# Where a small projection's weights are swept: from TensorE in the scan to VectorE in the feed-forward stages

## What is computed

```python
def ada_params(cond, w, b):                       # cond (1, 1024), w (1024, 6144), b (6144)
    m = jax.nn.silu(cond) @ w + b
    return jnp.split(m[..., None, :], N_MOD, axis=-1)

for i in range(DEPTH_2):                          # 2 layers
    sh_m, sc_m, gt_m, sh_f, sc_f, gt_f = ada_params(c, ada_w[i], ada_b[i])
    if kind == 0 or ctx_live:                     # layer 0 alone
        csh_m, csc_m, cgt_m, csh_f, csc_f, cgt_f = ada_params(c_ctx, ada_w[i], ada_b[i])
    h = modulate(x, norm_mix[i], sh_m, sc_m)      # rmsnorm(x, g) * (1 + scale) + shift
```

## Time and profile before

| | |
|---|---|
| runs | 2309.95, 2308.20, 2309.11 us; median 2309.11 |
| span of the profiled execution, first to last instruction | 2304.8 us |
| TensorE, VectorE, ScalarE, GpSimd busy | 91%, 27%, 20%, 11% of the span |
| bytes moved | 575.5 MB, 250 GB/s over the span |

### The profile page before, as it was taken

One profiled execution on the slowest core, in us unless ns is written; L12 is line 12 of the kernel. 1 busy time (PEld: TensorE's weight loads), 2 busy tenths in 40 slices (PEclk: granted clock), 3 DMA queues, 4 the chain that ended last, 5 costly groups with the idle time before them and its releaser, 6 DMA issues. The chain is left out here.

```text
span 2304.8 us, 25911 instructions
## 1 busy us (share of the span) xinstructions
PE 2107.9 (91%) x10718; PEld 1359.1 (59%) x10718; DVE 623.4 (27%) x1420; ACT 461.7 (20%) x899; POOL 252.8 (11%) x385
## 2 busy tenths in 40 slices
PE   8999899999999998878889998888889899998897
PEld 6854587678878755667674443333478644333334
DVE  4566340232213235743231110011111311111101
ACT  2222231222213345444320000000111200000001
POOL 2034120111112133000100000000000001000000
PEclk9999999999999999989889999999899899999998
DMA  7479644334432221110269999999924699999994
GB/s 251 146 325 412 249 146 146 109 128 146 146 99 73 74 73 37 37 38 2 110 248 380 428 428 427 427 427 428 380 100 154 280 379 427 428 428 427 428 428 188
DMA packets 105042, 575.51 MB, mean 250 GB/s; under 512 B 5536, under 2 KB 28665, under 8 KB 75225
## 3 DMA queue, kind: packets, MB, share of 16 engines
q1 hardware_dynamic: 103455, 570.59, 61.6%
q10 hardware_dynamic: 970, 2.23, 0.3%
q0 software_dynamic: 496, 0.97, 0.2%
HBM read 572.72 MB, written 1.05 MB: 249 GB/s over the span
## 5 line engine op out<-in xcount | busy, mean ns | idle before, releaser
L3094 PE MATMUL ex_u<-ring,ex_xt 128*64 128x512 f32 x1024 | 235.1, 614 | 29.2 <-DMA ring<-in_w 27.8
L3094 PE MATMUL ex_u<-ring_extra,ex_xt 128*64 128x512 f32 x1024 | 233.5, 610 | 28.5 <-DMA ring_extra<-in_w 28.5
L784 PE MATMUL linear_ps<-hT,ring 128*128 128x256 f32 x960 | 211.8, 383 | 8.5 <-PEq L444 6.4
L784 PEld LDWEIGHTS linear_ps<-hT,ring 128*128 128x128 f32 x960 | 184.4, 193 | 35.5 <-issue 8.5
L3094 PEld LDWEIGHTS ex_u<-ring,ex_xt 128*64 128x64 f32 x1024 | 82.6, 141 | 178.2 <-issue 178.1
L3094 PEld LDWEIGHTS ex_u<-ring_extra,ex_xt 128*64 128x64 f32 x1024 | 80.5, 141 | 178.7 <-issue 178.1
L2151 PE MATMUL dl_front<-dn_src,ring 128*128 128x256 f32 (+1 forms) x512 | 176.5, 501 | 2.4 <-DVE dp_cv L2318 2.4
L3200 DVE TENSOR_TENSOR ex_hid<-ex_sil,ex_u 128x512 f32<-128x512 f32 x32 | 34.8, 1086 | 490.0 <-PE ex_u L3094 490.0
L1570 PE MATMUL ffn_ps<-hT,ring 128*128 128x256 f32 x704 | 153.9, 382 | 4.3 <-PEq L677 4.3
L1570 PEld LDWEIGHTS ffn_ps<-hT,ring 128*128 128x128 f32 x704 | 134.9, 192 | 23.3 <-issue 4.7
L2151 PEld LDWEIGHTS dl_front<-dn_src,ring 128*128 128x128 f32 x512 | 99.4, 199 | 65.1 <-issue 57.6
(11 more groups left out here) (617 smaller groups left out, 2679.5 us busy)
## 6 DMA issues: line engine op xcount, KB each, us to landing
ring_extra<-in_w SPq DMA_DIRECT2D x88, 2048.0 KB, 25.4
ring<-in_w SPq DMA_DIRECT2D x88, 2048.0 KB, 25.5
ring<-in_ada_w SPq DMA_DIRECT2D x16, 2048.0 KB, 15.9
ring<-in_ffn_w_up SPq DMA_DIRECT2D x22, 1024.0 KB, 6.5
ring<-in_w_in SPq DMA_DIRECT2D x8, 2048.0 KB, 9.2
ring<-in_ada_w SPq DMA_DIRECT2D x16, 1024.0 KB, 14.7
ring<-in_w_in_a SPq DMA_DIRECT2D x8, 2048.0 KB, 8.5
ring<-in_w SPq DMA_DIRECT2D x16, 1024.0 KB, 7.2
```

The costliest lines, as they stand in the source:

```text
L784: mm = pe.matmul(ps[:, q % banks, 0:n], w[:, k, j * P:(j + 1) * P], src[:, k, 0:n], start=k == 0, stop=k == kc - 1)
L3094: mm = pe.matmul(u[H * a:H * a + H, i, :], xt[:, b, k, H * a:H * a + H], cols, start=k == 0, stop=k == KC - 1, skip_group_check=True)
```

## The change

Layer 0's 12 ada tiles stay in the scan. Layer 1's 12 are taken out of the scan and the stick-breaking stage, with the second row copy and turn. They are queued between the feed-forward weights, and VectorE sweeps them: in 48 steps of 128x1024 it multiplies each weight row by its partition's value of silu(c) and adds it to one array of 128x6144 (K.cond, Sweep.step). 22 steps stand in the up stage, one behind each chunk's convolution; 26 in the down stage, 4 ahead of the context's move, 10 behind it, and 12 behind context.scale. Then TensorE sums over the partitions (12 products with a column of ones, Sweep.sum, ahead of the last six f), ScalarE copies the row, TensorE turns it after c = 1, and VectorE finishes mods and gains of layer 1 after c = 3. A slot that held a swept tile is free when its four steps are done (K.swept_at).

With U0 to U10 for the tiles of w_up, D0 to D5 for those of w_down and S0 to S11 for the swept ones, the queue is now U0 S0 U1 U2 S1 U3 U4 S2 U5 U6 S3 U7 U8 S4 U9 U10 S5 D0 S6 S7 D1 S8 S9 D2 S10 S11 D3 D4 D5. By the rule of the slots U3 waits for S0, U5 for S1, U7 for S2, U9 for S3, D0 for S4, D1 for S5, S8 for D0, S9 for S6, D2 for S7, S10 for D1, S11 for S8, D3 for S9, D4 for D2, D5 for S10.

```diff
@@ issue @@
             if before >= 0:
-                sp.wait_ge(self.products.sem, self.done_at[before])
+                if before in self.swept_at:
+                    sp.wait_ge(self.counter("ada_swept").sem, self.swept_at[before])
+                else:
+                    sp.wait_ge(self.products.sem, self.done_at[before])
@@ stage_stick_breaking, TensorE and VectorE @@
             make_scores(0)
-            ada_multiply(pe, 0)
             make_scores(1)
-            ada_multiply(pe, 1)
             for i in range(pairs):
                 sum_later(i)
                 if i + 2 < pairs:
                     make_scores(i + 2)
-                if i + 2 < ada_tiles:
-                    ada_multiply(pe, i + 2)
                 mix(i)
-            for n in range(pairs + 2, ada_tiles):
-                ada_multiply(pe, n)
-            ada_turn(pe, 1)
...
-            ada_move(dve, 1, lambda out, x: dve.tensor_copy(out, x))
@@ stage_ssm_scan @@
-                if i + ADA_FRONT < ADA_SCAN:
+                if i + ADA_FRONT < ADA:
                     ada_multiply(pe, i + ADA_FRONT)
@@ stage_ffn_up, VectorE and SyncE @@
                         else:
                             ins.then_inc(conved.sem, conved.tick())
+                sweep.step(dve, c)
...
-            K.issue(sp, g0 + FC // per)
+            K.issue(sp, K.sweep_tiles[SWEPT_UP // 4])
@@ stage_ffn_down, TensorE, ScalarE, VectorE @@
+            pe.wait_ge(context.rooted.sem, context.rooted.at(1))
+            sweep.sum(pe, row_ps)
+            down = -(-FC // per)
...
             for c in range(KC):
+                if c == 2:
+                    sweep.turn(pe, turned_ps)
...
             context.shift_rows(act)
+            sweep.move(act, row_ps)
...
+            sweep.prepare(dve)
+            for q in range(SWEPT_UP, SWEPT_UP + 4):
+                sweep.step(dve, q)
             context.move_rows(dve)
+            for q in range(SWEPT_UP + 4, SWEPT_UP + 14):
+                sweep.step(dve, q)
             context.scale(dve)
+            for q in range(SWEPT_UP + 14, SWEEPS):
+                sweep.step(dve, q)
             for c in range(KC):
                 rn.cross_lengths(dve, c)
+                if c == 3:
+                    sweep.finish(dve, turned_ps)
@@ queue_first_block @@
-    for g in range(ADA_SCAN):
+    for g in range(ADA):
         queue_ada(K, g)
     queue_columns(K, io["ssm_w_glu"][0], 512)
-    for g in range(ADA_SCAN, 2 * ADA):
-        queue_ada(K, g)
...
+        if c % 4 == 0:
+            queue_sweep(K, c // 4)
...
+        for t in range(6 + f // 2, min(8 + f // 2, ADA)):
+            queue_sweep(K, t)
@@ class Sweep @@
+    def step(self, dve, q):
+        K = self.K
+        t, m = divmod(q, 4)
+        g = K.sweep_tiles[t]
+        if m == 0:
+            dve.wait_ge(K.landed[K.slot[g]], K.need[g])
+        w = K.ring[K.slot[g]][:, SWEEP * m:SWEEP * (m + 1)]
+        k, to = (2 * (t // 3) + t % 3, SWEEP * m) if t % 3 < 2 else (2 * (t // 3) + m // 2, SLOT + SWEEP * (m % 2))
+        acc = self.acc[:, to:to + SWEEP]
+        if k == 0:
+            ins = dve.tensor_scalar(acc, w, K.cond[:, k:k + 1], None, ALU.mult)
+        else:
+            dve.wait_ge(self.swept.sem, q)
+            ins = dve.scalar_tensor_tensor(out=acc, in0=w, scalar=K.cond[:, k:k + 1], in1=acc, op0=ALU.mult, op1=ALU.add)
+        ins.then_inc(self.swept.sem, self.swept.tick())
...
+    def sum(self, pe, ps):
+        pe.wait_ge(self.swept.sem, SWEEPS)
+        pe.wait_ge(self.added.sem, self.added.at(2))
+        for j in range(ADA):
+            part = j % 4
+            mm = pe.matmul(ps[32 * part:32 * part + 32, :], self.sel[:, 30 - 2 * j:62 - 2 * j], self.acc[:, 512 * j:512 * j + 512],
+                           start=j < 4, stop=j >= 8, tile_position=(0, 32 * part), skip_group_check=True)
```

More of the change, by code:

```diff
@@ L1346, in stage_glu, with stage_merge @@
     linear_stage(K, yT, 4, evac, kc=4, beside=lambda st: ({}, {}, programs))
-def stage_merge(K, o_attn, o_ssm, gates, dst, mem, finish):
+def stage_merge(K, o_attn, o_ssm, gates, dst, mem):
     nc = K.nc
@@ L1375, in _ @@
             own = K.own["dve"]
-            finish(dve)
+            added = K.counter("ada_added")
+            ada_finish(K, 0, K.ada["t_ps"], added, added.at(0))(dve)
             for c in range(KC):
@@ L1547, in stage_cross, with stage_ffn_up @@
     K.used = g0 + tiles
-def stage_ffn_up(K, src, hid, context):
+def stage_ffn_up(K, src, hid, context, sweep):
     nc = K.nc
@@ L1554, in stage_ffn_up @@
     g0, per = K.used, 2
+    of = [g for g in range(g0, len(K.tiles)) if g not in K.sweep_tiles]
+    tiles = of[FC // per] - g0
     with K.stage() as st:
@@ L1612, in _, with stage_ffn_down @@
         def _(sp):
-            K.issue(sp, g0 + FC // per)
-    K.used = g0 + FC // per
-def stage_ffn_down(K, hid, rn, setup, context):
+            K.issue(sp, K.sweep_tiles[SWEPT_UP // 4])
+    K.used = g0 + tiles
+def stage_ffn_down(K, hid, rn, setup, context, sweep):
     nc = K.nc
@@ L1621, in stage_ffn_down @@
     g0, per = K.used, 4
-    tiles = -(-FC // per)
+    of = [g for g in range(g0, len(K.tiles)) if g not in K.sweep_tiles]
+    tiles = of[-(-FC // per)] - g0
     turned = 4 * per
@@ L1627, in stage_ffn_down @@
         context.begin(st)
+        sweep.room(st)
         block = st.enter_context(nc.Block())
         at = lambda c: ps[:, c % 4, c // 4, :]
+        row_ps, turned_ps = context.ps[:, 0, :], context.ps[:, 1, 0:2 * 4 * ADA]
         @block.tensor
@@ L1643, in _ @@
                 mm.then_inc(full.sem, full.tick())
-                K.done_at[g0 + f // per] = full.count
-            last = [K.tile(pe, g0 + t, min(per, FC - t * per)) for t in range(turned // per, tiles)]
+                K.done_at[of[f // per]] = full.count
+            pe.wait_ge(context.rooted.sem, context.rooted.at(1))
+            sweep.sum(pe, row_ps)
+            down = -(-FC // per)
+            last = [K.tile(pe, of[t], min(per, FC - t * per)) for t in range(turned // per, down)]
             for c in range(KC):
+                if c == 2:
+                    sweep.turn(pe, turned_ps)
                 if c >= 4:
@@ L1653, in _ @@
                 mm.then_inc(full.sem, full.tick())
-            for t in range(turned // per, tiles):
-                K.done_at[g0 + t] = full.count
+            for t in range(turned // per, down):
+                K.done_at[of[t]] = full.count
             rn.sum_lengths(pe, ps)
@@ L1757, in first_block_ffn @@
         hid = K.sb("ffn_hid", [P, FC, T], ctx=K.part)
-        stage_ffn_up(K, K.hT, hid, context)
-        stage_ffn_down(K, hid, Renorm(K, (K.hT, room), gain("norm_ffn_post"), dst, pre, shift=shift), setup, context)
+        sweep = Sweep(K, K.part)
+        stage_ffn_up(K, K.hT, hid, context, sweep)
+        stage_ffn_down(K, hid, Renorm(K, (K.hT, room), gain("norm_ffn_post"), dst, pre, shift=shift), setup, context, sweep)
 def ada_setup(K):
@@ L1843, in ada_conditions, with ada_finish @@
             act.activation(c[:, :, 30 + v], K.params[:, K.cols[name]:K.cols[name] + KC], ACT.Silu).then_inc(silued.sem, silued.tick())
-def ada_finish(K):
-    added = K.counter("ada_added")
-    t_ps = K.ada["t_ps"]
+        act.activation(K.cond[:, :], K.params[:, K.cols["c"]:K.cols["c"] + KC], ACT.Silu)
+def ada_finish(K, l, t_ps, added, first):
     def finish(dve):
-        for l in range(2):
-            b0 = K.cols[f"ada_b{l}"]
-            for v in range(2):
-                at = 2 * 4 * ADA * l + v
-                dve.tensor_tensor(K.mods[l][:, v, :], t_ps[:, at:at + 2 * 4 * ADA - 1:2], K.params[:, b0:b0 + 6 * KC],
-                                  ALU.add).then_inc(added.sem, added.tick())
-        dve.wait_ge(added.sem, added.at(4))
-        for l in range(2):
-            for v in range(2):
-                for i, (name, scale) in enumerate(((f"norm_mix{l}", 1), (f"norm_ffn{l}", 4))):
-                    g = K.cols[name]
-                    dve.scalar_tensor_tensor(out=K.gains[l][:, v, i, :], in0=K.mods[l][:, v, scale * KC:(scale + 1) * KC],
-                                             scalar=1.0, in1=K.params[:, g:g + KC], op0=ALU.add, op1=ALU.mult)
-    return finish
@@ new lines, in finish @@
+        b0 = K.cols[f"ada_b{l}"]
+        for v in range(2 - l):
+            dve.tensor_tensor(K.mods[l][:, v, :], t_ps[:, v:v + 2 * 4 * ADA - 1:2], K.params[:, b0:b0 + 6 * KC],
+                              ALU.add).then_inc(added.sem, added.tick())
+        dve.wait_ge(added.sem, first + 2 - l)
+        for v in range(2 - l):
+            for i, (name, scale) in enumerate(((f"norm_mix{l}", 1), (f"norm_ffn{l}", 4))):
+                g = K.cols[name]
+                dve.scalar_tensor_tensor(out=K.gains[l][:, v, i, :], in0=K.mods[l][:, v, scale * KC:(scale + 1) * KC],
+                                         scalar=1.0, in1=K.params[:, g:g + KC], op0=ALU.add, op1=ALU.mult)
```

81 lines of the change are left out of this document (57 added, 24 removed).

## The result

The changed kernel took 2331.35 us (median of 4 runs) beside 2308.65 for the kernel before on the same chip: ratio 1.0105, 95% interval 1.0078 to 1.0132. It is slower by 22.7 us; 20.5 were forecast.

What follows compares the result with a forecast made beforehand. It took TensorE, busy for 91% of the span, as the bound. Front +3.2 and feed-forward part +17.3 gave +20.5 us on 2309.1: 2329.6 us, slower by 0.9%, range 2312 to 2339.

Steps and rivals of the forecast that it cites:

- Down's waits: Down stage: TensorE waits for D2 near f = 8, 3.9 us, and for D3 near f = 12, 5.1 us.
- The cold starts behind them: Down stage: each of the two waits costs TensorE a cold start, 3.6 us together (0 to 4.5).
- Sum and turning: Down stage: 2.9 us for the sum over partitions and 1.1 for the turning, 4.0 added on TensorE.
- The change of stage: End of up: the last step beside GpSimd's product holds up the start of down by 0.7 us (0 to 1.3).
- Up without a wait: Up stage: a step fits in each chunk and tiles land with 1.5 us to spare, so no stall.
- rival C: Up stage stalls too: five tiles come late by 1 to 2 us each, total 2338 to 2342; chance 0.07.
- Stick-breaking: Stick-breaking stage: 1.7 us won at its end, 5.4 lost to three clock drops on the path (0 to 9).
- The rival that the clock holds: TensorE's clock holds through the holes, so the cold starts fall away: 2318.8 us; chance 0.10.
- the row at 253.53: Stick-breaking: a mix before which a hole of 2.34 us had kept the clock, cited for 0 to 5 drops.
- The scan: Late scan steps: VectorE's waits for TensorE go, 2.3 us won (0 to 2.5).
- one drop of the clock that GLU's first products pay: End of the scan: TensorE, left with output products only, drops its clock once, 1.8 us lost (0 to 3.6).

Runs made afterwards that it cites:

- e1: The changed kernel with S9's four sweep steps moved ahead of context.scale: 2328.4 us, ratio 1.0071 to the kernel before.
- e9: The changed kernel with S9's steps ahead of the scaling, S7's ahead of the context's move, and the context's rows turned before f = 4, not 2: ratio 1.0088.
- e4: The changed kernel's front alone: nothing is swept, layer 1's vectors are the bias alone: 2315.1 us, ratio 1.0027 to the kernel before.
- e5: The changed kernel with one swept tile queued behind each w_up tile and two steps behind each of up's first 21 convolutions: 2319.0 us, ratio 1.0035.
- e3: The changed kernel with eight unread filler products at each of six places in stick-breaking: 2326.5 us, ratio 1.0070 to the kernel before.
- e6: The changed kernel with filler products in stick-breaking and four more in each of five late scan steps: 2326.5 us, ratio 1.0070.
- e8: The changed kernel with all sweep steps and the sum in up, plus filler in the scan and stick-breaking: 2301.7 us, ratio 0.9964.

## Why the prediction was right, point by point

**Down's waits.** Forecast 3.9 and 5.1 us, measured 3.57 and 5.12, at the places named, f = 8 and f = 12. The second has the chain forecast for it, shown by e1. The first has too (three tiles behind D0's end: 17.7 us forecast, 17.4 measured from S8's issue to the sums), with one link wrong: D2 left late because of S7's steps, which GpSimd's work beside them and S6's had held up by 3.1 us. By e9 that link decides nothing.

**The cold starts behind them** are the term that was mis-sized: 3.6 forecast, by two cold starts of 1.8 from the merge. Measured 6.76 - 3.62 = 3.1 for the sums and 16.23 - 13.9 = 2.3 behind the second, 5.5 together. The forecast's own upper bound was 4.5. *The Trainium skill, "TensorE: Matmul & The Clock Gate", section "HAM oscillation — how this bites in real kernels", has each wait for a weight tile followed by a cold start of the next; both waits here agree.*

**Sum and turning**: 4.0 forecast; from start to start 2.7 and 0.8. **The change of stage**: 0.7 forecast, 158.99 - 158.47 = 0.5 measured, gone in e4 and e5, by the means that the forecast named: GpSimd's last product takes 1.25 us beside the step, not 0.72. (The 1.472 that it took for a step beside GpSimd is the mean of two; the one beside GpSimd took 1.66, and steps there take up to 3.26.) **Up without a wait**: so it was, and the 1.5 us to spare are 1.2 to 1.8 from landing to use. They can be used up: in e3 three of the tiles land too late, at a cost of 0.9 us, which is rival C in small. Up and down together grew by 18.5 us, 17.3 were forecast.

**Stick-breaking**: 5.4 - 1.7 = +3.7 forecast, +3.0 in the profiled run, +3.5 between the means (40.0 and 36.5). Both halves were right in size: with the clock kept (e6) the 1.7 are there, without it they are lost more than three times over. The loss doesn't come as three cold starts of 1.8 us, by which the forecast priced it, but as stretches at half clock in which each short step takes longer: sums 1.65 us for 0.91, mixes 1.13 for 0.66. The rival that the clock holds is wrong; it was the row at 253.53 that spoke for it, a hole that by itself had not cost the clock.

**The scan** is the step that failed, in its account. Forecast were 2.3 us won by the late steps, and one drop of the clock that GLU's first products pay, 1.8. GLU pays nothing: from its first product to the first scores it is 8.43 us before and 8.44 after. The drops come in the steps themselves, two or three of them, and the output products at 3.50 us take back all that the steps win. The two errors were nearly equal: -0.5 forecast for both, and 38.3 against 38.2 us behind layer 0's last ada tile measured. That this part of the sum came out is luck. By e6, one execution, the 2.3 were right at full clock.

**The sum.** +20.5 forecast and +21.2 in the span of the profiled run, of which 1.2 stood there already at the first drive (134.31 for 133.08), ahead of what the change touches; behind the renorm's sums, where it touches nothing either, the run is 1.4 shorter. The stages between have +21.3: 18.5 in up and down, 2.8 in the front.

## What to carry to other kernels

A slot of a ring is a place in a queue: before a tile is put into one, ask who frees it, what stands ahead of that on its engine, and what is issued behind it. VectorE had room for all 48 steps and the stream for all 25 MB; two tiles in the wrong place cost 14 us of waits and half clock, and another order with the same work had none of either behind down's first products.

Work that fills an engine's holes is not free to remove where that engine's clock depends on it: here 48 fp32 products that stood in holes kept the granted clock of a chain of short steps at 1.00 and 0.95 in two profiles, and without them it was 0.70 to 0.80 in seven and the stage 3.5 us longer, although a copy and a turning had gone with them. The next stage lost little by it, 219.2 us in the mean of seven for 218.9, since it started at half clock before too (3.30 us); with filler and without the turning it starts at full clock, and two us are won there, a part of which up gives back. When useful work leaves, look at the granted clock of the stretch that it leaves, and put other useful work there, as the sum at the change of stage.

## What the runs showed of the hardware

- The same instructions took 38.0 to 42.0 us in stick-breaking and 85.2 to 87.8 us in the scan, by where the clock fell to 1.2 GHz. *The Trainium skill, "TensorE: Matmul & The Clock Gate", section "What's actually happening", has the number of cold products of one kernel vary between executions; these seven agree.* A difference of 2 us in such a stage needs several profiles.
- The length of one hole doesn't decide the clock: one of 2.73 us in e6 stands ahead of output products at 2.4 GHz (1.91), one of 2.73 in e8 ahead of the same products partly at 1.2 GHz (2.84), one of 2.52 in the changed kernel ahead of the same at 1.2 GHz (3.50), and one of 3.35 there ahead of a mix at full clock (0.66). Why one execution meets the half clock where another doesn't is not settled by these runs.
- The step of the sweep, a scalar_tensor_tensor of 128x1024 with a scalar by partition, takes 1.28 us in up and 1.33 in a row of twelve, each waiting for the one before. *The Trainium skill, "VectorE: DVE Perf Modes", section on the TRN2 errata, gives 1.13 by its table and 1.22 by the larger fixed term that it reports as measured, both estimates; no such step here is that short.* (The first six, tensor_scalar, take 0.74.)
- VectorE's steps and GpSimd's products lengthen each other. In the changed kernel the gated product takes 1.25 us beside a step, 0.72 before; a step beside a sum into hT takes 3.26. The form decides: in up the gated product keeps its 0.73 beside the six tensor_scalar steps, which read one tensor, and takes 1.25 beside each of the 16 scalar_tensor_tensor steps, which read two. In e5 the second such step behind a convolution takes 1.63 us, the first 1.28.
